# Forty instead of thirty-two tokens on fetched expert rows in a two-layer encoder kernel

## The reference

```
q = (xt @ wq).reshape(T, 8, 2, 128)
s = einsum('thpc,phnc->thpn', q, subkeys)        # 128 keys per half
top_s, top_i = top_k(s, 16)                      # per token, head, half
best_s, best_pos = top_k(all 16x16 sums, 16)     # 16 experts per token and head
expert = first_key * 128 + second_key            # one of 16384
g = softmax(best_s)
hid = gelu(einsum('td,thkd->thk', xt, u[expert]))
out = einsum('thk,thkd->td', g * hid, v[expert])
```

## Time and profile before

| | us |
|---|---|
| median of 3 runs | 2048.75 |
| lowest, highest | 2047.99, 2051.69 |
| the profiled execution | 2048.55 |
| its span (first to last instruction) | 2046.8 |
| TensorE busy | 2032.6 (99%) |
| VectorE busy | 1628.2 (80%) |
| ScalarE busy | 1242.8 (61%) |
| GpSimd busy | 853.0 (42%) |

### The profile page before, as it was taken

The page is one execution under the profiler, slowest core; times in us unless marked ns, Lnnn a source line. Parts: engine busy times, 40 slices in busy tenths (PEclk is TensorE's granted clock), DMA queues, the critical chain, the costliest instruction groups (busy, mean ns, idle before and its releaser), DMA issues.

```text
span 2046.8 us, 40235 instructions
## 1 busy us (share of the span) xinstructions
PE 2032.6 (99%) x14054; PEld 1877.7 (92%) x14054; DVE 1628.2 (80%) x2766; ACT 1242.8 (61%) x2055; POOL 853.0 (42%) x470
## 2 busy tenths in 40 slices
PE   9999999999999999999999999999999999999999
PEld 7877889999999999999988778899999999999998
DVE  5867877987888688888868678679788886888887
ACT  5855545467888555444568555554688885544444
POOL 2300005988887722122013000069888877221220
PEclk9999999999999999999999999999999999999999
DMA  7444564556555688999754445645565556998995
GB/s 250 150 153 146 182 195 155 195 195 209 194 186 180 213 315 311 308 311 316 243 199 156 149 147 183 203 153 195 195 207 196 180 186 224 316 315 302 313 313 193
DMA packets 122895, 446.85 MB, mean 218 GB/s; under 512 B 13968, under 2 KB 13968, under 8 KB 122256
## 3 DMA queue, kind: packets, MB, share of 16 engines
q1 hardware_dynamic: 102528, 371.24, 53.8%
q0 software_dynamic: 18432, 67.12, 10.1%
q10 hardware_dynamic: 1808, 6.89, 1.0%
HBM read 443.10 MB, written 1.05 MB: 217 GB/s over the span
## 4 chain that ended last, share of the span: by engine, by line
PE 93%; DVE 4%; ACT 2%; issue 1%; DMA 0%; DVEq 0%; ACTq 0%
PE ps L1008 21%; PE ps L610 17%; PE ps L611 17%; PE ps L612 17%; PE ps L1010 10%; PE ps L618 3%; PE ps L974 3%; PE ps L620 1%; PE ps L629 1%; DVE w_lo L1489 1%; PE ps L934 1%; PE ps L755 1%; ACT w_hi L1099 1%; PE ps L828 0%; PE ps L714 0%
## 5 line engine op out<-in xcount | busy, mean ns | idle before, releaser
L1008 PE MATMUL ps<-wgt,w_hi 128*128 128x448 f32 x2048 | 642.1, 374 | 0.0
L612 PE MATMUL ps<-hT,w_lo 128*128 128x224 f32 x2048 | 561.3, 274 | 0.0
L611 PE MATMUL ps<-hT,w_hi 128*128 128x224 f32 x2048 | 561.2, 274 | 0.0
L610 PE MATMUL ps<-hT,w_hi 128*128 128x224 f32 x2048 | 560.5, 274 | 0.0
L1010 PE MATMUL ps<-wgt,w_lo 128*128 128x224 f32 x2048 | 541.2, 264 | 0.0
L1308 ACT ACTIVATE w_hi<-raw 128x1024 fp32r<-128x1024 f32 x512 | 516.2, 1047 | 8.7 <-PE ps L612 5.8
L557 POOL TENSOR_TENSOR w_lo<-raw,w_hi 128x1024 fp32r<-128x1024 f32 x176 | 422.9, 2420 | 71.8 <-ACT w_hi L1308 70.6
L1008 PEld LDWEIGHTS ps<-wgt,w_hi 128*128 128x128 f32 x2048 | 384.1, 188 | 29.1
L612 PEld LDWEIGHTS ps<-hT,w_lo 128*128 128x128 f32 x2048 | 393.2, 192 | 0.0
L611 PEld LDWEIGHTS ps<-hT,w_hi 128*128 128x128 f32 x2048 | 392.8, 192 | 0.0
L610 PEld LDWEIGHTS ps<-hT,w_hi 128*128 128x128 f32 x2048 | 392.8, 192 | 0.0
(11 more groups left out here) (224 smaller groups left out, 2999.3 us busy)
## 6 DMA issues: line engine op xcount, KB each, us to landing
raw<-in_w_u SPq DMA_DIRECT2D x256, 512.0 KB
raw<-in_w_v SPq DMA_DIRECT2D x256, 512.0 KB
raw<-in_stream SPq DMA_DIRECT2D x192, 512.0 KB
arena<-in_bias ACTq DMA_DIRECT2D x2, 1024.0 KB, 5.5
arena<-in_subk ACTq DMA_DIRECT2D x2, 1024.0 KB, 4.9
x<-in_x SPq DMA_DIRECT2D x4, 256.0 KB, 4.8
arena<-x ACTq DMA_DIRECT2D x8, 128.0 KB, 3.0
arena<-in_gain_rows ACTq DMA_DIRECT2D x2, 512.0 KB, 6.0
```

The costliest lines, as they stand in the source:

```text
L610: mm(out_, left[0], right[0], start=start, stop=False, skip_group_check=group)
L611: mm(out_, left[0], right[1], start=False, stop=False, skip_group_check=group)
L612: return mm(out_, left[1], right[0], start=False, stop=stop, skip_group_check=group)
L1008: mm(ps[:, c, 0:2 * DENSE], w_hi[:, 2 * k + e, dims], wgt[:, k, e, :, :].rearrange("p a b -> p (a b)"), start=first, stop=False, skip_grou ...
```

## The change

`FETCHED` = 40 tokens are fetched, `DENSE` falls to 216 and the groups from 56 to 54. The eight more tokens lie in 16 parts of 8 partitions: one gather holds 16 experts for each of the eight, so 8 more gathers of `u` and 8 of `v` serve them, against their own token tile `xs_more` and their own sum. The row numbers of these eight are brought to the partitions by a matmul with a spread identity (`spread_keys`), a copy by ScalarE (`take_more`) and seven small operations of VectorE (`more_rows`) behind pair 2. The fill has 15 dots instead of 7. The v phase has 25 dots as before and 40 sums, two of them in every fourth pair. The parts of the eight tokens' sum are added by eight matmuls of 8 columns. `subT` moves to another place, and its transfer to a later one.

```
-SPARSE = 32
-DENSE = T - SPARSE
+SPARSE, MORE = 32, 8
+FETCHED = SPARSE + MORE
+DENSE = T - FETCHED
...
-GATHERS = 2 * SPARSE
-FILL_DOTS = (8, 14, 21, 29, FILL - 3, FILL - 2, FILL - 1)
+GATHERS = 2 * FETCHED
+MORE_PARTS = P // MORE
+SUM_ORDER = [*range(SPARSE, FETCHED), *range(SPARSE)]
+FILL_DOTS = (8, 10, 12, 15, 17, 19, 22, 24, 27, 29, 32, 34, FILL - 3, FILL - 2, FILL - 1)
...
+TWICE = [FIRST_SUM + 2 + 4 * i for i in range(MORE)]
+STEPS += sorted([FILL + FIRST_SUM + i for i in range(FETCHED - len(TWICE))] + [FILL + p for p in TWICE])
...
                     if pair == 4:
                         pool.wait_ge(rows_known.sem, rows_known.at(layer, 1))
+                        pool.wait_ge(more_known.sem, more_known.at(layer, 1))
...
-                                       [h[:, kc, SPARSE:T] for h in (hT_hi, hT_lo)],
+                                       [h[:, kc, FETCHED:T] for h in (hT_hi, hT_lo)],
...
+                def spread_keys():
+
+                    pe.wait_ge(more_spread.sem, more_spread.at(layer, 1))
+                    mm(ps[:, 4, 0:3 * P], spread_more, rt_tok[:, 0, :, :].rearrange("p a b -> p (a b)"),
+                       start=True, stop=True)
+                    mm(ps[:, 4, 3 * P:3 * P + 1], spread_more, rstd[:, 0:1], start=True, stop=True
+                       ).then_inc(more_mm.sem, 1)
...
+                for c in range(KC):
+                    mm(ps[:, c, 2 * DENSE:2 * DENSE + MORE], xs_more[:, c * P:(c + 1) * P], token_of[:],
+                       start=False, stop=False, skip_group_check=True)
...
+                act.dma_start(subT[:].rearrange("p a b -> p (a b)"),
+                              subk[bass.ds(layer, 1), :, :].rearrange("a p n -> p (a n)")
+                              ).then_inc(subk_loaded.sem, 16)
                 for j in range(PARTS):
                     act.dma_start(xs[j * SPARSE:(j + 1) * SPARSE, :], x[0:SPARSE, 0, :]).then_inc(xs_loaded.sem, 16)
+                for j in range(MORE_PARTS):
+                    act.dma_start(xs_more[j * MORE:(j + 1) * MORE, :], x[SPARSE:FETCHED, 0, :]).then_inc(xs_loaded.sem, 16)
                 act.wait_ge(squared.sem, squared.at(layer, 4))
...
+                def take_more():
+
+                    act.wait_ge(more_mm.sem, more_mm.at(layer, 1))
+                    f(copies, ps[:, 4, 0:3 * P + 1], ACT.Copy).then_inc(more_copied.sem, 1)
...
                 for t in range(TT):
                     take_route(t)
+                take_more()
...
+                    own.one(v.tensor_tensor(xs_more, xs_more, ring[0], ALU.mult).then_inc(dve_chain, 1))
...
+                def more_rows(layer=layer):
+
+                    dve.wait_ge(more_copied.sem, more_copied.at(layer, 1))
+                    own.one(v.tensor_reduce(part_of, ident[:].rearrange("p (j t) -> p j t", j=MORE_PARTS), AX.X, ALU.add
+                                            ).then_inc(dve_chain, 1))
+                    dve.wait_ge(dve_chain, own.n)
+                    own.one(v.tensor_tensor(picks, copies[:, 0:3 * P].rearrange("p (c j s) -> p c j s", c=3, j=MORE_PARTS),
+                                            part_of.unsqueeze(1).unsqueeze(3).broadcast_to([P, 3, MORE_PARTS, MORE]),
+                                            ALU.mult).then_inc(dve_chain, 1))
...
+                    v.tensor_scalar(row_of[:, SPARSE:FETCHED], numbers, float(layer * KEYS * KEYS), None, ALU.add
+                                    ).then_inc(more_known.sem, 1)
...
-                    if u in STEPS:
-                        dot(STEPS.index(u))
+                    if u in FILL_DOTS:
+                        dot(FILL_DOTS.index(u))
+                    if u == 2:
+                        more_rows()
```

More of the change, by code:

```diff
@@ L208, in build @@
         bias = view(BIAS, B_HEADS, T)
-        subT = view(BIAS, 16, P)
+        subT = view(YT, 16, P)
         sq = view(QKT, 8, 512)
@@ L242, in build @@
         G = view(0, KEYS, DENSE)
-        spare = [view(KEYS * DENSE + D * i, D) for i in range(RING + 1)]
-        xs, ring = spare[2], spare[:2] + spare[3:]
+        spare = [view(KEYS * DENSE + D * i, D) for i in range(RING + 2)]
+        xs_more, xs, ring = spare[0], spare[3], spare[1:3] + spare[4:]
+        copies = ring[1][:, 0:3 * P + 1]
+        picks = ring[1][:, 512:512 + 3 * P].rearrange("p (c j s) -> p c j s", c=3, j=MORE_PARTS)
+        spread_more = ring[2][:, 512:512 + P]
+        picked = ring[2][:, 0:3 * MORE].rearrange("p (c s) -> p c s", c=3)
+        numbers = ring[2][:, 3 * MORE:4 * MORE]
+        part_of = ring[2][:, 4 * MORE:4 * MORE + MORE_PARTS]
         v_low = view(0, 8, DENSE)
         expert = ps[0:SPARSE, 0, 256:256 + P]
-        row_of = route[:, 0, 0:SPARSE].bitcast(U32)
-        share = route[:, 1, 0:SPARSE]
-        hid = qk_rs[:].rearrange("p a b -> p (a b)")[:, 0:SPARSE]
-        scale_of = ya_rs[:, 0, 0:1]
+        row_of = route[:, 0, 0:FETCHED].bitcast(U32)
+        share = route[:, 1, 0:FETCHED]
+        hid = qk_rs[:].rearrange("p a b -> p (a b)")[:, 0:FETCHED]
+        scale_of, scale_more = ya_rs[:, 0, 0:1], ya_rs[:, 1, 0:1]
         outT = view(8 * DENSE, 8, T)
@@ L967, in _ @@
                             route_transposes(e)
+                        if k == 1 and e == 0:
+                            spread_keys()
                 def gate_group(n, k):
@@ L1280, in _ @@
                         take_yb(0)
-                act.dma_start(subT[:].rearrange("p a b -> p (a b)"),
-                              subk[bass.ds(layer, 1), :, :].rearrange("a p n -> p (a n)")
-                              ).then_inc(subk_loaded.sem, 16)
                 take_probT(15)
@@ L1387, in weigh_hot @@
                         row = hot[n % 2][:, q, 1, :]
-                        last = f(row, row.bitcast(F), ACT.Copy, scale=route_hi[:, SPARSE + 4 * n + q:SPARSE + 4 * n + q + 1].bitcast(F))
+                        last = f(row, row.bitcast(F), ACT.Copy, scale=route_hi[:, FETCHED + 4 * n + q:FETCHED + 4 * n + q + 1].bitcast(F))
                     last.then_inc(hot_weighted.sem, 1)
@@ L2019, in landed @@
                     dve.wait_ge(signal.sem, signal.at(layer, 16 * (q // RING + 1)))
+                def more_rows(layer=layer):
[6 more added lines that the diff above has]
+                                            ALU.mult).then_inc(dve_chain, 1))
+                    own.one(v.tensor_copy(scale_more, copies[:, 3 * P:3 * P + 1]).then_inc(dve_chain, 1))
+                    dve.wait_ge(dve_chain, own.n)
+                    own.one(v.tensor_reduce(picked, picks.rearrange("p c j s -> p c s j"), AX.X, ALU.add).then_inc(dve_chain, 1))
+                    dve.wait_ge(dve_chain, own.n)
+                    own.one(v.scalar_tensor_tensor(out=numbers, in0=picked[:, 0, :], scalar=float(KEYS), in1=picked[:, 1, :],
+                                                   op0=ALU.mult, op1=ALU.add).then_inc(dve_chain, 1))
+                    own.one(v.tensor_copy(share[:, SPARSE:FETCHED], picked[:, 2, :]).then_inc(dve_chain, 1))
+                    dve.wait_ge(dve_chain, own.n)
+                    v.tensor_scalar(row_of[:, SPARSE:FETCHED], numbers, float(layer * KEYS * KEYS), None, ALU.add
+                                    ).then_inc(more_known.sem, 1)
                 def dot(s):
@@ L2091, in _ @@
                         share_out()
-                    if FILL + p in STEPS:
-                        q = STEPS.index(FILL + p)
-                        if q < SPARSE:
+                    for q in [q for q in range(GATHERS) if STEPS[q] == FILL + p]:
+                        if q < FETCHED:
                             dot(q)
                         else:
-                            add_rows(q - SPARSE)
+                            add_rows(q)
                     for j in {LAST_SUM + 1: (0,), LAST_SUM + 2: (1,), LAST_SUM + 3: (2, 3)}.get(p, ()):
```

54 lines of the change are left out of this document (34 added, 20 removed).

## The result

The changed kernel takes 2081.62 us (median of 4 runs, 2078.53 to 2086.84) against 2048.49 us (2047.99 to 2051.69) for the kernel before: a ratio of 1.0163, 95% interval 1.0151 to 1.0176. It is 33 us slower. The forecast was 2053.0 with a range to 2062, so the side was right and the size was not. Its four runs lie 8 us apart, those of the kernel before 4 us. The profiled execution took 2081.68 us, with a span of 2079.9.

The account below looks back on a forecast made before the run. TensorE, always busy in the early part and v phase, was taken as the bound: 2048.55 - 17.4 + 0.5 + 13.8 + 3.0 + 4.0 - 0.4 + 0.6 + 0.3 = 2053.0 us; range 2038 to 2062.

Parts of the forecast that it names:

- the query stall: Before query 4, TensorE waits for sixteen small transfers issued by ScalarE at 0.65 us each: 6.9 us a layer, 13.8 in all.
- I take 8.5 ns: -17.4 us: V phase: each of 2048 matmul pairs gets 8.5 ns shorter with 432 + 216 columns instead of 448 + 224, -17.4 us.
- at the edge; 0: V phase: second sums in every fourth pair raise transfers to 348 GB/s against 344 at full share; 0, up to +4.
- the lower bound of 6.7 ns: V phase: if only the wide matmul's 16 columns count, each pair saves 6.7 ns, 13.7 us in all.
- rival D: V phase bound by transfers in its 32 pairs of double sums: 1.9 us per layer, 2057 us; chance 0.10.
- the eight closing products: End of each layer: eight added matmuls of 8 columns at 111.6 ns, 0.9 us per layer.
- The clock's price: First queries after TensorE's stand run at half pace: 1.5 us per layer, +3.0, between 0 and 4.
- Rival A: Small transfers ahead of the queries are issued fast, 0.37 us each; stalls 5 us, kernel 2042 us; chance 0.24.
- The wait before pair 5: Fill: gathers wait for the late row numbers, 2.0 us beyond the slack, +4.0 for two layers; 1 to 7.
- rival B: U phase: columns count there too, 3.3 ns for each of 6144 matmuls, 20.5 us more saved, 2032.5 us; chance 0.07.
- rival C: Fill: VectorE and GpSimd, locked against each other by every dot, lose 1 us per dot: 2077, or 2061; chance 0.09.
- the two groups less: TensorE: two groups of four matmuls less per layer, 0.12 us per matmul plus the wider stream, -1.9 us in all.

## Why the prediction was wrong

The sum missed 28.6 us. Half of it is the v phase, where the gain of the columns was put too high and the transfers at nothing; a quarter is the size of the query stall, and a quarter lies in the fill and the early part.

**v phase: the step that failed first.** "I take 8.5 ns: -17.4 us" and "at the edge; 0". The columns gave 5.8 ns a pair, 11.8 us, even less than the lower bound of 6.7 ns: 5.6 us off. Averaged over some 450 pairs of layer 0, the start of the wide matmul to that of the narrow one went from 212 to 210 ns, and from there to the next wide one from 101 to 97.5, so neither of the two pictures behind the bounds (all columns count; only the wide one's) is what happened. The rate of 348 GB/s was worked out rightly and set against 344 at a full share, and then priced at 0 with a chance of 0.10 for more. It is 6.7 us in the profiled execution (rival D, priced 3.8), 5.9 by the mean of the recorded v phases. The rest, 1.8 us, is that the eight closing products were counted as eight instructions of 0.11 us where the profile has sixteen. In all 14.1 us.

**Queries: right in place and kind, off in size.** The first copy was to come near 292 and came at 295.08; the wait was 10.1 us, not 6.9. The issues cost what was said, 0.66 us each at their fastest. What was left out is that issues behind the 1 MB load take longer: `subT` got 0.4 us, and its place costs some 2.6 more. With it out of the way the wait is the 6.9 us of the prediction (7.3 and 6.7). The clock's price was 2.5 and about 1.2 us, against 1.5. In all 7.3 us. Rival A, fast issues, had a chance of 0.24 and was wrong.

**Fill and early part.** The wait before pair 5 came where and how it was forecast, at 2.2 and 2.7 us for 2.0. The clock behind it was not thought of (1.6 us), nor was the loss of about 1 us a layer by the dot behind pair 19, where -0.2 was taken for all dots. VectorE's second multiplication with the gain, in the early part, was not costed at all: it holds one of three splits (8.77 us instead of 7.93 for the same three) and TensorE stands 0.7 us. And the matmuls on the row numbers take 0.8 us, not 0.3: two instructions of 384 columns are 0.32 us each. In all 7.5 us for both stages and layers.

The Trainium skill, page "FP8 and Floating Point Precision", section "TensorE Precision Notes", gives true fp32 as four passes. The trace agrees with it: 0.65 us for 384 columns is 1.7 ns a column, four times 1 / 2.4. The dense matmuls are of the reduced kind (fp32r in the rows), and I had priced the new ones like them.

**What held.** No gain from columns in the u phase: the early part is 124.0 us with 216 columns alone and the spacing 111.7 ns, as before, so rival B falls, and the formula that it leans on does not describe this stream, in which each matmul has its own weight load. The dots' small cost in the changed kernel held, though in the kernel before rival C's lock costs 4.4 us a layer for seven dots, and so did the transfers ahead of the queries as the largest new cost. Nearly all terms were off in the same direction; only the two groups less gave more, 3.0 us of the fill instead of 1.9. With every cost at the upper end that the prediction itself gave, the sum is 2048.6 - 13.7 + 0.5 + 18 + 4 + 7 + 5 + 0.6 + 0.3 + 4 = 2074, still below the measured time: the bounds were too narrow one by one, and the range, to 2062, did not reach the sum of the upper ones.

## What to carry to other kernels

A transfer costs time on the engine that issues it: count the issues ahead of an instruction with little slack, look at what large load stands ahead of them on the same queue, and give them to an engine that is waiting, if what lands later for it is not needed soon. Where a schedule asks for more bandwidth than any stretch of the trace has held for long, price it as a wait and spread the transfers before adding any; the average of the phase left room, the 32 pairs did not. When a wait is removed on one engine, look at who is locked against it: the 2.2 us before pair 5 passed from GpSimd to VectorE unchanged, and only moving the work to idle time paid.

## What the runs showed of the hardware

- TensorE's clock fell to 0.51 behind a wait of 2.2 us in layer 0 and stayed at 1.00 behind one of 2.7 us at the same place in layer 1. The length of the wait alone does not decide it, and no run here shows what does.
- A GpSimd split and a VectorE operation on 8 columns with two operands in SBUF exclude each other: 2.51 us instead of 0.17.
- An issue of a small transfer takes 0.63 us on ScalarE and 0.53 on GpSimd. On ScalarE single ones took up to 3.0 us with a 1 MB load ahead and GpSimd issuing beside it.
- The u phase's matmuls are 111.7 ns apart at 224 and at 216 columns, the scores' 111.6 at 128. A pair of 448 and 224 columns takes 313.4 ns and one of 432 and 216 takes 307.6, where 16 columns at one per cycle would be 6.7 ns and 24 would be 10.
- With eight doubled sums the v phase took 317.8 to 323.8 us (fourteen layers); with them left out or fed by the other gathers 317.3 each time; with four doubled dots and four doubled sums 317.3 to 318.4 (six layers). What sets the wait near the limit of the transfers was not tried.
